# A three-layer transformer block kernel whose opening loads, turns, scales and splits half chunks of x and one contraction tile of the first weight unit ahead of the rest

## The reference

```python
def rmsnorm(x, g):
    xf = x.astype(jnp.float32)
    y = xf * lax.rsqrt(jnp.mean(xf * xf, axis=-1, keepdims=True) + RMS_EPS)
    return (y * g.astype(jnp.float32)).astype(x.dtype)

def swiglu(h, w_gate, w_up, w_down):
    return (jax.nn.silu(h @ w_gate) * (h @ w_up)) @ w_down

x = x + 0.5 * swiglu(rmsnorm(x, norm_ffn1[l]), w_ffn1_gate[l], w_ffn1_up[l], w_ffn1_down[l])
```

## Time and profile before

| | |
|---|---|
| runs, us | 895.38, 895.74, 895.93 |
| span of the profiled execution, us | 893.9 |
| own time of the profiled execution, us | not given apart from the runs; the median of the runs lies 1.84 above the span |
| PE busy | 877.1 us, 98% of the span |
| DVE, ACT, POOL busy | 66%, 54%, 11% |
| DMA | 157.25 MB at a mean of 176 GB/s; 300 to 263 GB/s in the first slices |

### The profile page before, as it was taken

One profiled execution on the slowest core, in us unless ns is written; L12 is line 12 of the kernel. 1 busy time (PEld: TensorE's weight loads), 2 busy tenths in 40 slices (PEclk: granted clock), 3 DMA queues, 4 the chain that ended last, 5 costly groups with the idle time before them and its releaser, 6 DMA issues.

```text
span 893.9 us, 14996 instructions
## 1 busy us (share of the span) xinstructions
PE 877.1 (98%) x5261; PEld 730.5 (82%) x5261; DVE 589.0 (66%) x912; ACT 481.5 (54%) x729; POOL 95.8 (11%) x93
## 2 busy tenths in 40 slices
PE   8999999999999999999999999999999999999996
PEld 5788888878677778888888878777888999999985
DVE  4755555566689876655555567899766767667685
ACT  6544444447466746444444466666756455445465
POOL 5220000011000011000000022662011000000030
PEclk9999999999999999999999999999999999999999
DMA  9886666555653354755565537443256655655521
GB/s 300 262 263 199 211 199 199 169 154 165 208 181 130 96 165 142 226 196 187 178 199 188 181 103 241 137 166 109 87 160 200 209 190 166 193 191 179 186 74 48
DMA packets 121963, 157.25 MB, mean 176 GB/s; under 512 B 9983, under 2 KB 82947, under 8 KB 121920
## 3 DMA queue, kind: packets, MB, share of 16 engines
q1 hardware_dynamic: 119648, 151.65, 52.2%
q0 software_dynamic: 1760, 4.41, 2.0%
q10 hardware_dynamic: 512, 0.61, 0.2%
HBM read 155.56 MB, written 1.07 MB: 175 GB/s over the span
## 4 chain that ended last, share of the span: by engine, by line
PE 89%; DVE 6%; ACT 3%; issue 2%; ACTq 0%; DVEq 0%
PE bank L513 23%; PE bank L515 22%; PE bank L514 22%; PE bank L546 4%; PE bank L545 4%; PE bank L544 4%; DVE w_lo L1903 2%; PE bank L806 1%; PE bank L627 1%; PE bank L1029 1%; PE bank L1005 1%; ACT w_hi L1333 1%; PE bank L1017 1%; PE bank L890 0%; PE bank L858 0%
## 5 line engine op out<-in xcount | busy, mean ns | idle before, releaser
L1910 DVE TENSOR_TENSOR w_lo<-w_raw,w_hi 128x1024 fp32r<-128x1024 f32 x179 | 219.1, 1224 | 175.5 <-ACT w_hi L1342 175.4
L1342 ACT ACTIVATE w_hi<-w_raw 128x1024 fp32r<-128x1024 f32 x180 | 190.3, 1058 | 207.1 <-PE bank L515 172.2
L513 PE MATMUL bank<-w_hi,x_hi 128*128 128x512 f32 (+1 forms) x688 | 275.6, 401 | 3.3 <-DVE w_lo L1903 1.2
L515 PE MATMUL bank<-w_hi,x_lo 128*128 128x512 f32 (+1 forms) x688 | 267.2, 388 | 0.0
L514 PE MATMUL bank<-w_lo,x_hi 128*128 128x512 f32 (+1 forms) x688 | 266.6, 387 | 0.0
L513 PEld LDWEIGHTS bank<-w_hi,x_hi 128*128 128x128 f32 x688 | 129.2, 188 | 33.7 <-issue 6.8
L1903 DVE TENSOR_TENSOR w_lo<-w_raw,w_hi 128x1024 fp32r<-128x1024 f32 x99 | 123.8, 1270 | 42.3 <-ACT w_hi L1333 42.0
L515 PEld LDWEIGHTS bank<-w_hi,x_lo 128*128 128x128 f32 x688 | 129.1, 188 | 27.4
L514 PEld LDWEIGHTS bank<-w_lo,x_hi 128*128 128x128 f32 x688 | 129.5, 188 | 23.5
L1333 ACT ACTIVATE w_hi<-w_raw 128x1024 fp32r<-128x1024 f32 x100 | 103.4, 1054 | 40.7 <-PE bank L515 33.6
L513 PE MATMUL bank<-w_hi,h_hi 128*128 128x512 f32 x272 | 107.6, 396 | 1.1 <-DVE h_lo L2027 0.5
(11 more groups left out here) (302 smaller groups left out, 816.4 us busy)
## 6 DMA issues: line engine op xcount, KB each, us to landing
w_raw<-in_w_ffn_gate SPq DMA_DIRECT2D x132, 256.0 KB, 2.9
w_raw<-in_w_ffn_up SPq DMA_DIRECT2D x132, 256.0 KB, 3.1
w_raw<-in_w_ffn_down SPq DMA_DIRECT2D x132, 256.0 KB, 3.0
w_raw<-in_w_in SPq DMA_DIRECT2D x104, 256.0 KB, 3.0
w_raw<-in_w_out SPq DMA_DIRECT2D x32, 256.0 KB, 3.3
w_raw<-in_w_ple_gate SPq DMA_DIRECT2D x16, 256.0 KB, 3.2
arena<-bias_rows POOLq DMA_DIRECT2D x8, 256.0 KB, 4.6
w_raw<-in_cmp_w_k SPq DMA_DIRECT2D x8, 256.0 KB, 3.5
```

The source lines that it names most:

```text
L513: pe.matmul(out_, hi, wh, start=start, stop=False)
L515: return pe.matmul(out_, lo, wh, start=False, stop=stop)
L1342: act.activation(whi[:, slot * UNIT:(slot + 1) * UNIT], raw[:, slot * UNIT:(slot + 1) * UNIT], ACT.Copy).then_inc(sem("hi_done"), 1)
L1910: dve.tensor_tensor(wlo[:, s_], raw[:, s_], whi[:, s_].bitcast(F32), ALU.subtract).then_inc(sem("lo_done"), 1)
```

## The change

- **x, first two chunks in halves.** Chunks 0 and 2 are loaded as two DMAs of 128 x 256 each (`x_half`). The first halves signal `x0_first` and `x2_first`; the second halves signal `x_in0` and `x_in2`.
- **Unit 0 by contraction tile.** Four DMAs of 128 KB (`load_first`): gate and up of tile 0 (signal `w_first`), then the second half of chunk 0, then gate and up of tile 1 (signal `landed0`). Before, it was two DMAs of 256 KB.
- **ACT's four small row loads** move to SP's queue, behind the issue of unit 3.
- **PE**: `warm(6)` in place of `warm(9)`; turns the first halves of chunks 0 and 2 (two transposes each); `warm(7)`; in `opening` the six matmuls of tile 0 for m = 0 and m = 1; then the turning of both second halves; then the six matmuls of tile 1; then the third chunk's turning and the rest as before from (0,1) on.
- **ACT**: round the first half of chunk 0, `whi` of tile 0, round the first half of chunk 2, `whi` of tile 1, round the two second halves, then split unit 1 and on as before.
- **DVE**: scale the two first halves, `wlo` of tile 0, scale the two second halves, `wlo` of tile 1, then unit 1 and on as before.
- **POOL**: four low parts of halves in place of two of chunks.
- Some semaphores are merged elsewhere (`tabx` into `warm_in`, `phi_done`, `plo_done` and `pT_full` into `p_turned`, `root_ready` into `qr_done`, `lam_done` into `lamt`, `gain0_in` into `con_in`), with the counts moved accordingly.

```diff
+            def load_first(wg, wu, kk, signal):
+                for half, w in enumerate((wg, wu)):
+                    sp.dma_start(raw[:, kk * 512 + half * HID:kk * 512 + (half + 1) * HID],
+                                 w[kk * P:(kk + 1) * P, 0:HID]).then_inc(sem(signal), 16)
...
-                    load_gu((base + j) % RING, wg, wu, j, slice(0, HID))
+                    if first and j == 0:
+                        load_first(wg, wu, 0, "w_first")
+                        to, of = x_half(0, 1)
+                        sp.dma_start(to, of).then_inc(sem("x_in0"), 16)
+                        load_first(wg, wu, 1, "landed0")
+                    else:
+                        load_gu((base + j) % RING, wg, wu, j, slice(0, HID))
                     if first and j == 1:
                         x_load(1)
                         x_load(3)
+                if first:
+                    for to, r0, nr, src in row_loads[:4]:
+                        sp.dma_start(to[r0:r0 + nr, :], src).then_inc(sem("rows_act"), 16)
...
+            def first_turn(c, h):
+
+                for k in range(2 * h, 2 * h + 2):
+                    m, n = divmod(X_ORDER[c], 2)
+                    at = m * D + n * 512 + k * P
+                    mm = pe.transpose(bank[norm_bank(0, c)][:, k * P:(k + 1) * P], x[:, at:at + P], ident)
+                return mm
+
             def opening():
 
-                for m, j in ((0, 0), (1, 0), (0, 1), (1, 1), (0, 2), (0, 3), (1, 2), (1, 3)):
-                    if j % 2 == 0:
+                for kk in range(2):
+                    for m in range(M):
+                        if kk == 0:
+                            pe.wait_ge(sem(X_FIRST[m]), PARTED)
+                            pe.wait_ge(sem("w_first"), W_PARTED)
+                        elif m == 0:
+                            pe.wait_ge(*lo_ready(1))
+                        c = slice(kk * 512, (kk + 1) * 512)
+                        last = three(bank[m][:, :], xT(xhi, kk, m), xT(xlo, kk, m), whi[:, c], wlo[:, c], kk == 0, False)
+                    if kk == 0:
+                        for c in range(2):
+                            pe.wait_ge(sem(f"x_in{X_ORDER[c]}"), 16)
+                            first_turn(c, 1).then_inc(sem("nt_full"), 1)
+                last.then_inc(sem("w_used"), 1)
+                norm_chunk(0, 2)
+                for m, j in ((0, 1), (1, 1), (0, 2), (0, 3), (1, 2), (1, 3)):
+                    if j != 3:
                         pe.wait_ge(sem("xlo_done"), 2 * (j // 2) + m + 1)
...
-            warm(9)
-            pe.wait_ge(sem("con_in"), 16)
-            pe.wait_ge(sem("gain0_in"), 16)
+            warm(6)
+            pe.wait_ge(sem("con_in"), 32)
             pe.transpose(bank[4][:, 0:8], rows_a[0:8, :], ident[0:8, 0:8]).then_inc(sem("gain0_full"), 1)
             for c in range(2):
-                norm_chunk(0, c)
+                pe.wait_ge(sem(X_FIRST[c]), LANDED)
+                first_turn(c, 0).then_inc(sem(X_FIRST[c]), 1)
             warm(7)
...
-            act.dma_start(x_chunk(2), x_rows(2)).then_inc(sem("x_in2"), 16)
-            for to, r0, nr, src in row_loads[:4]:
-                act.dma_start(to[r0:r0 + nr, :], src).then_inc(sem("rows_act"), 16)
-            norm_hi(0, (0,))
-            split(0)
-            norm_hi(0, (1,))
+            for h, signal in enumerate(("x2_first", "x_in2")):
+                to, of = x_half(1, h)
+                act.dma_start(to, of).then_inc(sem(signal), 16)
...
+            first_hi(0)
+            act.wait_ge(sem("w_first"), W_LANDED)
+            act.activation(whi[:, 0:512], raw[:, 0:512], ACT.Copy).then_inc(sem("w_first"), 1)
+            first_hi(1)
+            act.wait_ge(sem("landed0"), 32)
+            act.activation(whi[:, 512:1024], raw[:, 512:1024], ACT.Copy).then_inc(sem("hi_done"), 1)
+            second_hi(0)
+            second_hi(1)
             split(1)
...
-            for c in range(2):
-                scaled(0, R_GAIN, c)
-            split(0)
...
+            first_scaled(0, 0)
+            first_scaled(1, 0)
+            dve.wait_ge(sem("w_first"), W_ROUNDED)
+            dve.tensor_tensor(wlo[:, 0:512], raw[:, 0:512], whi[:, 0:512].bitcast(F32), ALU.subtract
+                              ).then_inc(sem("w_first"), 1)
+            first_scaled(0, 1)
+            first_scaled(1, 1)
+            dve.wait_ge(sem("hi_done"), 1)
+            dve.tensor_tensor(wlo[:, 512:1024], raw[:, 512:1024], whi[:, 512:1024].bitcast(F32), ALU.subtract
+                              ).then_inc(sem("lo_done"), 1)
             split(1)
```

More of the change, by code:

```diff
@@ L392, in program, with x_half, half_T, half4 @@
         X_ORDER = (0, 2, 1, 3)
+        X_FIRST = ("x0_first", "x2_first")
+        LANDED, TURNED, SCALED, ROUNDED, PARTED = 16, 17, 18, 19, 20
+        W_LANDED, W_ROUNDED, W_PARTED = 32, 33, 34
+        def x_half(c, h):
+            m, n = divmod(X_ORDER[c], 2)
+            return (x[:, m * D + n * 512 + h * S:m * D + n * 512 + (h + 1) * S],
+                    t["x"][0, m * P:(m + 1) * P, n * 512 + h * S:n * 512 + (h + 1) * S])
+        def half_T(tensor, c, h):
+            return chunk_T(tensor, X_ORDER[c])[:, 2 * h:2 * h + 2, :]
+        def half4(c, h):
+            return bank4(norm_bank(0, c))[:, 2 * h:2 * h + 2, :]
         block = ctx.enter_context(nc.Block())
@@ L468, in blockload @@
                     load_cols((u + j) % RING, w, 2 * j, c0, width)
-            x_load(0)
+            to, of = x_half(0, 0)
+            sp.dma_start(to, of).then_inc(sem("x0_first"), 16)
             ffn(U_FFN1, t["w_ffn1_gate"][0], t["w_ffn1_up"][0], t["w_ffn1_down"][0], first=True)
@@ L728, in ple_turn @@
                                           av(PIN + m * 256 + k * P, [P]), ident)
-                mm.then_inc(sem("pT_full"), 1)
+                mm.then_inc(sem("p_turned"), 1)
             def ple_unit(k):
@@ L789, in ffn_conv @@
                 pe.wait_ge(sem("h_done"), 2 * n0 + 2 * STEPS)
-                pe.wait_ge(sem("plo_done"), 1)
+                pe.wait_ge(sem("p_turned"), 3)
                 ple_unit(0)
@@ L844, in bias_rows @@
             def bias_rows():
-                pe.wait_ge(sem("tabx"), 1)
+                pe.wait_ge(sem("warm_in"), 2)
                 pe.wait_ge(sem("tab_in"), 16)
@@ L1475, in ffn_conv @@
                 conv_mid(STEPS)
-                act.wait_ge(sem("pT_full"), 1)
-                act.activation(chunk_T(xhi, 3), bank4(6), ACT.Copy).then_inc(sem("phi_done"), 1)
+                act.wait_ge(sem("p_turned"), 1)
+                act.activation(chunk_T(xhi, 3), bank4(6), ACT.Copy).then_inc(sem("p_turned"), 1)
                 conv_gelu(STEPS)
@@ L1489, in _, with first_hi, second_hi @@
             act.dma_start(rows_a[0:8, :], t["norm_ffn1"].rearrange("a (k p) -> (a k) p", p=P)
-                          ).then_inc(sem("gain0_in"), 16)
-            act.dma_start(x_chunk(2), x_rows(2)).then_inc(sem("x_in2"), 16)
-            for to, r0, nr, src in row_loads[:4]:
-                act.dma_start(to[r0:r0 + nr, :], src).then_inc(sem("rows_act"), 16)
-            norm_hi(0, (0,))
-            split(0)
-            norm_hi(0, (1,))
+                          ).then_inc(sem("con_in"), 16)
+            for h, signal in enumerate(("x2_first", "x_in2")):
+                to, of = x_half(1, h)
+                act.dma_start(to, of).then_inc(sem(signal), 16)
+            def first_hi(c):
+                act.wait_ge(sem(X_FIRST[c]), SCALED)
+                act.activation(half_T(xhi, c, 0), half_T(xg, c, 0), ACT.Copy).then_inc(sem(X_FIRST[c]), 1)
+            def second_hi(c):
+                act.wait_ge(sem("xg_done"), c + 1)
+                act.activation(half_T(xhi, c, 1), half_T(xg, c, 1), ACT.Copy).then_inc(sem("xhi_done"), 1)
+            first_hi(0)
[6 more added lines that the diff above has]
+            second_hi(1)
             split(1)
@@ L1818, in _ @@
             split(U_IN2 + 31 + RING)
-            act.activation(sm(QR + 8, 8), sm(QMS, 8), ACT.Sqrt).then_inc(sem("root_ready"), 1)
+            act.activation(sm(QR + 8, 8), sm(QMS, 8), ACT.Sqrt).then_inc(sem("qr_done"), 1)
             quad_squares(1)
-            act.wait_ge(sem("root_ready"), 1)
+            act.wait_ge(sem("qr_done"), 2)
             quad_root(1)
@@ L2058, in ffn_conv @@
                 conv_taps(STEPS)
-                dve.wait_ge(sem("phi_done"), 1)
+                dve.wait_ge(sem("p_turned"), 2)
                 dve.tensor_tensor(chunk_T(xlo, 3), bank4(6), chunk_T(xhi, 3).bitcast(F32), ALU.subtract
-                                  ).then_inc(sem("plo_done"), 1)
+                                  ).then_inc(sem("p_turned"), 1)
                 conv_mul(STEPS)
@@ L2099, in _, with first_scaled @@
             dve.wait_ge(sem("gain0_done"), 1)
-            for c in range(2):
-                scaled(0, R_GAIN, c)
-            split(0)
+            def first_scaled(c, h):
+                if h:
+                    dve.wait_ge(sem("nt_full"), c + 1)
```

(27 more changed lines are left out.)

5 lines of the change are left out of this document (2 added, 3 removed).

## The result

The changed kernel took 897.77 us (median of nine runs, 895.92 to 898.51) beside 895.74 for the kernel before (nine runs, 895.38 to 896.56). The ratio is 1.0018, 95% interval 1.001 to 1.0026: slower by 0.18%. I had forecast 898.0, within 896.5 to 899.4. The nine runs lie in two groups: 895.92 and 896.13, and seven from 897.51 up to 898.51. The profiled execution, 897.77 with a span of 895.9, is of the upper group, so all that follows is read from that group.

What follows compares the result with a forecast made beforehand. PE, busy 877.1 of 893.9 us, was taken as the bound, with the opening's chain over ACT and DVE. Silu 1.4 later at T0 8.4, plus 0.9 for the clock, gave +2.3: 898.0 us, range 896.5 to 899.4.

Steps and rivals of the forecast that it cites:

- What bounds the kernel: From 15.62 to 28.99 the chain runs over DVE and ACT; an earlier PE start helps only if they are earlier too.
- T0: When PE starts its dense work after the change: near 9.3 with slow fillers, 8.4 at best, against 10.34 before.
- 8.4: T0 with fast fillers, summed over turning, scaling, rounding and tile 0's low parts: 1.9 before 10.34.
- The loads don't set this: Claim that loads do not fix T0: chunk 2's first half lands between 6.0 and 6.9, taken as 6.0.
- 0.9: Cost of the clock at the seven later fillers, moving T0 from 8.4 to near 9.3; bounds 0 and 2.1.
- The clock: Six first fillers and a gap may leave PE at 1.2 GHz, so the seven later fillers delay T0 by 0.9.
- Behind T0: Second halves turned behind tile 0's matmuls make ACT wait; Silu at T0 + 13.9, 22.3 to 23.2 against 20.90.
- The loads and the moved row loads: Units 1 and 4 issued 1.4 and 3.2 later on SP, row loads needed only at 22 us: cost nothing.
- A: Rival: the clock has risen by 6.5 despite the gap, the rest stands: +1.4, 897.1; chance 0.33.
- F: Rival: PE's early start carries through past tile 1 and the second halves: -1.8, 893.9; chance 0.08 whole or in part.
- C: Rival: the clock is low through tile 0's matmuls too: 0.9 + 1.15 + 1.4, +3.5, 899.2; chance 0.14.
- D: Rival: chunk 2's first half lands at 6.9, T0 is 9.0: +2.0, 897.7; no own chance, within the forecast's range.

Runs made afterwards that it cites:

- e7: The kernel before with six first filler matmuls in place of nine, nothing else: median 896.27 us, ratio 1.0006 to the kernel before.
- e1: The changed kernel with nine first filler matmuls in place of six: median 896.98 us, ratio 1.0014 to the kernel before.
- e2: The changed kernel without the seven later fillers ahead of tile 0: median 898.68 us, ratio 1.0030 to the kernel before.
- e3: The changed kernel with the second halves turned ahead of tile 0's matmuls, behind the seven fillers: median 896.40 us, ratio 1.0002 to the kernel before.
- e4: The changed kernel with ACT splitting unit 1 ahead of rounding the two second halves: median 897.03 us, ratio 1.0010 to the kernel before.
- e8: The changed kernel itself, measured again without an edit: median 897.72 us, ratio 1.0016 to the kernel before.
- e5: The changed kernel with the edits of e1 and e3 together: median 895.30 us, ratio 0.9994 to the kernel before.
- e6: e5 with the seven later fillers cut to three ahead of the second halves' turning and two behind it: median 895.25 us, ratio 0.9993 to the kernel before.
- e9: The kernel of e6 measured again: median 895.23 us, ratio 0.9993 to the kernel before.

## Why the prediction was right

- **What bounds the kernel.** Right. From the Silu to the end it is 872.8 to 873.3 in all eleven profiled executions, with the Silu anywhere from 19.90 to 23.65. Nothing behind it gives time back or takes it. One reading was too strong. "If the start at 10.34 governed the rest, the chain would run over PE up to some 28 us. It doesn't": in the kernel before the chain does run over PE from 10.34 until the fourth chunk is turned, and passes to DVE only at 15.62. There an earlier start of PE was worth something, up to the 1.00 that ACT idles ahead of 16.35; in e7 PE began 0.78 earlier and the Silu came 0.75 earlier.

```profile
10.34 0.47 PE bank L513
...
15.15 0.45 PE bank L806 x4
```

- **T0.** Predicted 9.3, measured 8.89, and this is in part luck: two errors of opposite sign met. The first part of the sum, 8.4 without slow fillers, was 0.7 too late. Tile 0's low parts were there at 7.52, and with the handoff of 0.14 that e1 shows PE could have started at 7.66. The second part, the fillers, was 0.3 too small: they held PE until 8.89, 1.23 and not 0.9.
- **Why 8.4 was too late.** "The identity and the gain land as before: the turn of x begins at 5.34" failed: it began at 4.06. The nine fillers of before had held the turning by 0.2 at most, as the identity landed there at 4.94, 4.2 behind its issue, and the gain was turned at 5.14. What changed is the loads: chunk 0's 256 KB had landed 4.0 behind their issue, its first half 2.7, and in every kernel with half loads and six fillers (the changed one, e2, e3, e4, e8) the gain is turned at 3.86, where e7, with the loads of before, waits for the identity until 4.65. Whether the halves or the moved row loads do it was not tested. "The loads don't set this" failed too. Of the 1.3 of earlier turning most is lost again, because PE then waits 1.03 for chunk 2's first half, and DVE makes tile 0's low part only behind the scaling of that half. It landed at 5.73, and I had it at 6.0 or later.
- **Why 0.9 was too small.** The fillers started at 6.26 in place of 6.5, and all seven were slow, 3.03 with the last one's tail, where I had up to 2.96 (7 x 0.42 is 2.94) and a rise on the way.
- **The clock.** That the level was low when the later fillers ran is right in both profiled executions of the changed kernel; 15 of its 20 runs are in the upper group. By e1's median it is worth 0.8. The matmuls of the changed kernel are 0.43 apart up to 8.82 and 0.23 apart from 9.36 on. The Trainium skill's page "TensorE: Matmul & The Clock Gate", section "What's actually happening", says that activity releases the throttle, and the traces agree. As the granted clock reads 1.00 in the start of every trace, also where fillers are 0.42 apart, only the spacing told it.
- **Behind T0.** Predicted and measured distances: ACT goes on, T0 + 2.4 and 2.49; PE at tile 1, 3.5 and 3.44; unit 1 for m = 0, 5.5 and 5.91 (its `wlo` took 1.54 beside POOL, I had 1.23); unit 2, 9.7 and 9.91; the Silu, 13.9 and 13.89. `bias_rows` was predicted at 30.4 to 31.3 and stood at 30.87. This part of the sum, which holds most of the loss, was right by its mechanism: in e3 ACT resumes 0.97 earlier and the Silu comes 0.87 earlier, in e4 ACT fills its wait with unit 1 and the Silu comes 0.94 earlier behind the turning.
- **The loads and the moved row loads** cost nothing that shows: ACT has no wait for a load from 7.46 on in the profiled execution of the changed kernel. The place where they would show is unit 1, once ACT is early enough, as in e5.
- **Rivals.** A, with 0.33, is probably the low group, 5 of 20 runs, though at 896.1 it lies below my 897.1. An estimate: with fast fillers tile 0 could start at 7.66, or 0.33 earlier if chunk 2's first half lands as in e2, where it was turned at 5.45 and not 5.78; with 13.89 to the Silu, 873.1 behind it and the 1.87 by which the time of the profiled execution exceeds its span that is 896.2 to 896.5. F, the early start carried through, needed the turning ahead of the matmuls, which is e3's edit; with e1's and e6's, F became true for 0.5 to 0.8 of its 1.8. C was seen in part in e8, and in e4, where nearly all of tile 0's matmuls were slow. D failed: in the kernels with half loads chunk 2's first half was turned from 5.45 to 6.38, not at 6.9, and only its second half landed near 7.

## What to carry to other kernels

Starting the bounding engine earlier is worth what the chain of waits says, and here the chain ran over ACT's list: look which engine ends last some microseconds behind the start, and ask what in the new order that engine waits for. When work is cut in halves, the second half must be produced while the first is consumed, not behind it in the producer's list. Fillers that keep a clock are part of the critical path twice, by their length when the clock is low and by the clock when they are missing; do not shorten them together with another edit. Read how long a load takes from its landing, and not from when the engine that waits for it goes on.

## What the runs showed of the hardware

The granted clock in the trace is 1.00 from the first microsecond, also where 512-column matmuls start 0.42 to 0.43 apart, the 1.2 GHz level; after a fall inside the execution it is shown properly (0.50 in e2 from 9 to 15). The fall in e2 came when PE was already at work again, and the lower level lasted for over six microseconds.

When the level first rises differs between executions, although PE has done the same until then. e2's program is the changed kernel's up to the turning of chunk 2's first half. That turning takes 0.44 at 5.45 in e2, and 0.69 at 5.78 in the changed kernel. With nine first fillers the last of them is fast already in e6 and still slow in e9, the same kernel. The first line is e2's, the second e6's, the third e9's.

```profile
5.45 0.44 PE L666 MATMUL bank<-con,x 128*128 128x128 f32 x2 [0.70 <-DMA x<-in_x]
...
1.19 3.59 PE L906 MATMUL bank<-sg 128*128 128x512 bf16 x9 [1.19 <-DVE sg L2161]
...
1.19 4.02 PE L906 MATMUL bank<-sg 128*128 128x512 bf16 x9 [1.19 <-DVE sg L2161]
```

With six first fillers the later fillers ran 0.22 apart in one profiled execution (e7, with the loads of before) and 0.43 apart in four (the changed kernel, e3, e4, e8). With nine they ran 0.22 apart in all five (the kernel before, e1, e5, e6, e9). The 20 runs of the changed kernel fell into two groups with medians of 896.1 and 897.9 and none between 896.18 and 897.51.
